# Gate and up GEMMs of the four FFNs by Strassen's seven products instead of eight, one NeuronCore of a Trainium2

## The reference

```python
def swiglu(x, w_gate, w_up, w_down):
    return (jax.nn.silu(x @ w_gate) * (x @ w_up)) @ w_down

x = x + 0.5 * rmsnorm(swiglu(rmsnorm(x, gains[0]), w_gate, w_up, w_down), gains[1])
```

## Time and profile before

| | us |
|---|---|
| median of 3 runs | 2648.09 |
| lowest, highest | 2644.64, 2652.86 |
| span of the profiled execution | 2645.6 |
| TensorE busy | 2565.5 (97%) |
| VectorE, ScalarE, GpSimd busy | 1241.8, 873.3, 411.5 |

### The profile page before, as it was taken

The page is one execution under the profiler, slowest core; times in us unless marked ns, Lnnn a source line. Parts: engine busy times, 40 slices in busy tenths (PEclk is TensorE's granted clock), DMA queues, the critical chain, the costliest instruction groups (busy, mean ns, idle before and its releaser), DMA issues.

```text
span 2645.6 us, 51530 instructions
## 1 busy us (share of the span) xinstructions
PE 2565.5 (97%) x20533; PEld 2435.9 (92%) x20533; DVE 1241.8 (47%) x2018; ACT 873.3 (33%) x1542; POOL 411.5 (16%) x602
## 2 busy tenths in 40 slices
PE   8999999998998999999999999999989989999998
PEld 7999999995557999999999999999979969999998
DVE  5444325546664544432444442467546665444423
ACT  4222224114443422222422222344354444222322
POOL 0000003023331200000200000155245532000001
PEclk9999999999999999999999999999999999999999
DMA  4332322348994233233132233223210133322331
GB/s 125 87 89 86 107 82 65 81 130 287 299 307 152 64 88 88 87 103 88 56 88 87 87 106 90 65 65 87 67 35 1 33 105 96 88 87 87 101 88 45
DMA packets 397765, 263.17 MB, mean 99 GB/s; under 512 B 10984, under 2 KB 370613, under 8 KB 397608
## 3 DMA queue, kind: packets, MB, share of 16 engines
q1 hardware_dynamic: 386096, 223.03, 29.0%
q0 software_dynamic: 11536, 38.28, 4.4%
HBM read 251.71 MB, written 9.56 MB: 99 GB/s over the span
## 4 chain that ended last, share of the span: by engine, by line
PE 90%; DVE 3%; issue 2%; ACT 2%; POOL 2%; DMA 1%; POOLq 0%; SPq 0%; ACTq 0%; DVEq 0%
PE ps L495 70%; PE ps L481 5%; PE ps L1445 2%; PE ps L2391 2%; PE ps L2407 1%; PE ps L1502 1%; PE ps L1457 1%; POOL xT L1026 1%; PE ps L509 1%; PE ps L538 1%; PE ps L2415 1%; PE ps L1468 1%; DVE w_lo L473 0%; DVE rstd_rows L1051 0%; PE ps L2375 0%
## 5 line engine op out<-in xcount | busy, mean ns | idle before, releaser
L473 DVE TENSOR_TENSOR w_lo<-w_raw,w_hi 128x1024 fp32r<-128x1024 f32 (+1 forms) x314 | 423.4, 1348 | 971.3 <-ACT w_hi L466 969.5
L495 PE MATMUL ps<-hd_hi,w_hi 128*128 128x272 f32 x3712 | 772.0, 289 | 4.4 <-DVE w_lo L473 4.3
L495 PE MATMUL ps<-hd_lo,w_hi 128*128 128x272 f32 x3712 | 768.3, 288 | 0.0
L495 PE MATMUL ps<-hd_hi,w_lo 128*128 128x272 f32 x3712 | 762.7, 287 | 0.0
L466 ACT CAST w_hi<-w_raw 128x1024 fp32r<-128x1024 f32 (+1 forms) x314 | 351.4, 1119 | 1124.8 <-PE ps L495 1069.3
L495 PEld LDWEIGHTS ps<-hd_hi,w_hi 128*128 128x128 f32 x3712 | 580.8, 189 | 7.8 <-issue 7.6
L495 PEld LDWEIGHTS ps<-hd_lo,w_hi 128*128 128x128 f32 x3712 | 585.0, 189 | 0.0
L495 PEld LDWEIGHTS ps<-hd_hi,w_lo 128*128 128x128 f32 x3712 | 582.8, 188 | 0.0
L1026 POOL TENSOR_TENSOR xT<-xT,rstd_rows 128x272 f32<-128x272 f32 x96 | 84.5, 910 | 1708.3 <-DVE rstd_rows L1051 1708.2
L495 PE MATMUL ps<-h_hi,w_hi 128*128 128x272 f32 x1232 | 255.4, 289 | 0.0
L495 PE MATMUL ps<-h_lo,w_hi 128*128 128x272 f32 x1232 | 254.9, 288 | 0.0
(11 more groups left out here) (529 smaller groups left out, 2973.7 us busy)
## 6 DMA issues: line engine op xcount, KB each, us to landing
w_raw<-in_ffn_w_gate_dram SPq DMA_DIRECT2D x88, 512.0 KB, 3.7
w_raw<-in_ffn_w_up_dram SPq DMA_DIRECT2D x88, 512.0 KB, 3.8
w_raw<-in_ffn_w_down_dram SPq DMA_DIRECT2D x64, 704.0 KB, 4.6
v_pages<-in_cache_a_v_dram POOLq DMA_DIRECT2D x128, 256.0 KB, 4.5
w_raw<-in_c_w_in_dram SPq DMA_DIRECT2D x33, 512.0 KB, 4.0
k_pages<-in_cache_a_k_dram SPq DMA_DIRECT2D x64, 256.0 KB, 4.2
k_pages_raw<-in_cache_a_k_dram SPq DMA_DIRECT2D x64, 256.0 KB, 4.4
w_raw<-in_ab_w_in_dram SPq DMA_DIRECT2D x25, 512.0 KB, 3.9
```

Source lines behind the costliest of these rows:

```text
L473: e.tensor_tensor(w_lo[:, n % 2, 0:nk * P], raw[:, n % RAW, 0:nk * P], w_hi[:, n % 2, 0:nk * P].bitcast(F32), ALU.subtract).then_inc(sem(" ...
L495: mm = e.matmul(ps[:, bank + h, 0:TH], w, x[:, k0 + k, half(h)], start=first and k == 0 and w is wh and x is x_hi, stop=last and k == nk - ...
```

## The change

The first gate tile and the first up tile of each FFN (four units, 192 matmuls) stay as they were. The other 20 tiles of gate and of up are taken as 10 pairs each. One *pass* p (p = 0 to 19, even: gate pair, odd: up pair) multiplies a 2 x 2 block matrix of weights (two halves of K = 4 k tiles, two output tiles) with a 2 x 2 block matrix of rows (two halves of K, two halves of T) by Winograd's form of Strassen's scheme: seven products instead of eight, each 4 k tiles x 3 passes = 12 matmuls into one bank.

- **Rows.** Strassen adds up results of both halves of the rows, so they must have their 1/rms first. DVE computes 16 tiles `xn` = xT * gain * rb (128 x 272) into `x_sums`, GpSimd four sums of 128 x 1088 (`x_sum` 0 to 3), ACT and DVE split seven operands of 128 x 1088 (`x_part` 0 to 6). All this once for each FFN.
- **Weights.** Two DMAs of 512 KB bring the 128 x 8 x 256 block of a pass to `w_pair` (two buffers). GpSimd makes four sums of 128 x 512 (`w_sum`). ACT and DVE split the seven weight operands (`part`, 128 x 512) into a ring of five slots: part q+5 is made when product q is done.
- **Results.** Seven additions each pass: ACT copies product 0 out of PSUM (`p1`), DVE does `u_sum`, `w_sum`, `quarter` (128 x 272 each) and `sums` (128 x 544), two additions happen in PSUM (products 4 and 6 accumulate onto a bank that holds an earlier result, 5 too), ACT handles `corner`. After each odd pass a silu of 128 x 816 (`gates`) and a product of 128 x 1088 (`gated`) on DVE, for pairs 1 to 4 the split of 128 x 1088 (`pair_high` on ACT, `pair_low` on DVE); the last 12 tiles of the hidden rows are kept whole and split at the end of the stage (`late`), since the row operands occupy their place.
- The loop is written out; one semaphore for each engine counts all its steps of an FFN in a fixed order.

```diff
+PRODUCTS = (("a11", 0), ("s2", 1), ("s1", 3), ("s3", 2), ("a12", 0), ("s4", 3), ("a22", 2))
+        def pool_gate_up(e, g):
+            for n, (to, a, b, op) in enumerate(((2, 3, 6, ALU.add), (1, 2, 0, ALU.subtract), (3, 0, 3, ALU.subtract),
+                                                (5, 4, 1, ALU.subtract))):
+                wait_step(e, "vector", f, "xn", (7, 11, 11, 15)[n])
+                if n:
+                    wait_step(e, "gpsimd", f, "x_sum", n - 1)
+                e.tensor_tensor(x_sums[:, to, :, :], x_sums[:, a, :, :], x_sums[:, b, :, :],
+                                op).then_inc(sem("ffn_gpsimd"), did("gpsimd", "x_sum", n))
+            for p in range(WP):
...
+                pair_landed(e, f, p)
+                b11, b12, b21, b22 = (w_pair[x][:, k:k + KH, m:m + P] for k in (0, KH) for m in (0, P))
+                t3, t2 = (part_rows(w_sums[x][:, y, :]) for y in range(2))
+                e.tensor_tensor(t3, b22, b12, ALU.subtract).then_inc(sem("ffn_gpsimd"), did("gpsimd", "w_sum", 4 * p))
+                wait_step(e, "gpsimd", f, "w_sum", 4 * p)
+                e.tensor_tensor(t2, t3, b11, ALU.add).then_inc(sem("ffn_gpsimd"), did("gpsimd", "w_sum", 4 * p + 1))
+                e.tensor_tensor(b12, b12, b11, ALU.subtract).then_inc(sem("ffn_gpsimd"), did("gpsimd", "w_sum", 4 * p + 2))
...
+                wait_step(e, "vector", f, "part", PROD * p + 1)
+                e.tensor_tensor(t2, b21, t2, ALU.subtract).then_inc(sem("ffn_gpsimd"), did("gpsimd", "w_sum", 4 * p + 3))
+        def pe_product(e, g, q):
...
+            if name == "s4":
+                wait_step(e, "vector", f, "w_sum", p)
+            if name == "a22":
+                wait_step(e, "vector", f, "quarter", p)
+            wait_step(e, "vector", f, "part", q)
+            for k in range(KH):
+                for w, x in ((wh, xp_hi[idx]), (wh, xp_lo[idx]), (wl, xp_hi[idx])):
+                    mm = e.matmul(ps[:, bank, 0:TH], w[:, k * P:(k + 1) * P], x[:, k, :],
...
+        def dve_gate_up(e, g, s):
...
+            dve_rstd_x(e, s, first + 2)
+            dve_split(e, first + 3, 0, KD)
+            gate(0)
+            for h, parts in ((1, (3, 6)), (0, (0, 4))):
+                for k in range(KD):
+                    e.scalar_tensor_tensor(x_sums[:, parts[k // KH], k % KH, :], xT[:, k, half(h)], gain(l, n_pre, k),
+                                           rb[:, half(h)], ALU.mult, ALU.mult
+                                           ).then_inc(sem("ffn_vector"), did("vector", "xn", (1 - h) * KD + k))
+            up(0)
+            hidden(0)
+            low(0)
+            for n in range(3):
+                dve_x_part(e, g, n)
+            gate(1)
+            for q in range(3):
+                dve_part(e, g, q)
+            for n in (3, 4):
+                dve_x_part(e, g, n)
+                dve_part(e, g, n)
+            for q in range(PROD * WP):
+                p, idx = q // PROD, q % PROD
+                pairs = p // 2
+                product_done(e, f, q)
+                dve_sums(e, f, p, idx)
+                if idx == 0 and p % 2 == 0 and p:
+                    dve_gated(e, f, pairs)
+                if idx == 2 and p % 2 == 0 and 0 < pairs < LATE // 2:
...
+                if q + RING < PROD * WP:
+                    dve_part(e, g, q + RING)
+                if q < 2:
+                    dve_x_part(e, g, 5 + q)
+                if q == 0:
+                    up(1)
+                if q == 2:
+                    hidden(1)
+                if q == 4:
+                    low(1)
...
+            dve_gated(e, f, HP)
```

More of the change, by code:

```diff
@@ L568, in quads, with vector_steps @@
                 body(g["quads"] - 1, True)
-        def gate_up_count(g):
-            return KF * ffns.index((int(g["name"][-2]), int(g["name"][-1])))
+        def vector_steps():
+            steps = [("gate", 0), *(("xn", x) for x in range(2 * KD)), ("up", 0), ("hidden", 0), ("low", 0)]
+            steps += [*(("x_part", n) for n in range(3)), ("gate", 1), *(("part", q) for q in range(3))]
+            steps += [("x_part", 3), ("part", 3), ("x_part", 4), ("part", 4)]
+            for q in range(PROD * WP):
+                p, idx = q // PROD, q % PROD
+                steps += [(x, p) for x in {1: ("u_sum",), 2: ("w_sum",), 3: ("quarter",), 6: ("sums",)}.get(idx, ())]
+                steps += [("gated", p // 2)] * (idx == 0 and p % 2 == 0 and p > 0)
+                steps += [("pair_low", p // 2)] * (idx == 2 and p % 2 == 0 and 0 < p // 2 < LATE // 2)
+                steps += [("part", q + RING)] * (q + RING < PROD * WP)
+                steps += [("x_part", 5 + q)] * (q < 2) + [("up", 1)] * (q == 0) + [("hidden", 1)] * (q == 2) + [("low", 1)] * (q == 4)
+                steps += [("late", x) for x in late_at(q) if q < PROD * WP - 1]
+            return steps + [("gated", HP)] + [("late", x) for x in range(7, KF - LATE)]
@@ L603, in act_gate_up, with dve_late @@
+        def dve_late(e, f, x):
+            wait_step(e, "scalar", f, "late", x)
+            e.tensor_tensor(h_hi[:, LATE + x, :], h_raw[:, LATE + x, :], h_lo[:, LATE + x, :].bitcast(F32),
+                            ALU.subtract).then_inc(sem("ffn_vector"), did("vector", "late", x))
         def act_gate_up(e, g, s):
-            m0 = gate_up_count(g)
+            f, first = ffn_of(g), g["first"]
             if s == 0:
                 e.preload_act_table(ACT.Silu)
[L608 to L621, removed]
@@ new lines, in act_gate_up, with dve_gated @@
+            act_split(e, first + 5, 0, KU)
+            for x in range(9, KF - LATE):
+                act_late(e, f, x)
+        def dve_gated(e, f, i):
+            p = 2 * (i - 1)
+            wait_step(e, "vector", f, "sums", p + 1)
+            wait_step(e, "scalar", f, "gates", i)
+            wait_step(e, "scalar", f, "corner", p + 1)
+            to = up_buf if i < LATE // 2 else pair_tiles(h_raw, i)
+            e.tensor_tensor(to, gate_buf, up_buf, ALU.mult).then_inc(sem("ffn_vector"), did("vector", "gated", i))
@@ L3229, in _ @@
                 if kind == "ffn":
-                    sp_gemm(e, gemms[f"gate_up{l}{w}"])
-                    sp_gemm(e, gemms[f"down{l}{w}"])
+                    sp_gate_up(e, gemms[f"gate_up{l}{w}"], gemms[f"down{l}{w}"])
+                    sp_gemm(e, gemms[f"down{l}{w}"], after=1)
                 if kind == "ab":
```

350 lines of the change are left out of this document (294 added, 56 removed).

## The result

The changed kernel took 2667.86 us, the median of four runs (2667.11 to 2672.42); the kernel before took 2649.19 us (2644.64 to 2652.86, four runs). The ratio is 1.0072, 95% interval 1.0057 to 1.0087: slower by 0.7%. The forecast was 2642 us and "no change". The profiled span grew by 20.1 us, from 2645.6 to 2665.7 us, where the forecast had -6: the miss to explain is 26 us.

What follows compares the result with a forecast made beforehand. It took the number of TensorE's matmuls as the bound, other engines hidden. Fewer matmuls -120, start +62, first pass +30, even passes +16, clock +6 gave -6 us: 2648.1 to 2642 us, range 2590 to 2700.

Steps and rivals of the forecast that it cites:

- first pass and clock: Pass 0 of each FFN: ends 7.5 us late, 30 us in all, plus 6 us for TensorE's lowered clock after idling.
- rival 1: Gate and up stage: GpSimd's lock on DVE hardly costs; -84, 2564 us; shares 0.40 with less lock and lower terms.
- Start: Before product 0 of each FFN: TensorE idles 15 us, 17 in the first, until U + 27; 62 us over four.
- Even passes: Passes 2, 4, 6, 8: `quarter` some 1.0 us late, `w_sum` in time; 16 us over four FFNs.
- estimate of 2663 us: Start and passes: whole GpSimd instruction taken as the lock on DVE, +21 us, 2663 us.
- What costs nothing: End of the stage and waits: DVE and ACT free after product 134, down's first splits covered, satisfied waits free; 0 us.
- so I keep 125 ns: Products in all passes: matmuls keep the earlier trace's 125 ns, 1.5 us a product, 10.5 us a pass.
- up to 3 us each FFN: Start of down: the cost if its first unit's 8.3 us no longer covered DVE's work of about 5 us.
- Rival 2: All passes: DVE becomes the bound throughout; +116, 2758 us in full, about 2675 in part; shares 0.38 for slower.
- Rival 3: Start of each FFN: row sums of 2.7 us and a longer low clock; +31, 2673 us; shares 0.38 for slower.
- Rival 4: Products: matmuls fall out of time, for instance from fetching written-out code; 2% slower pace, +19 us; shares 0.38.
- terms that come out higher: Whole sum: the forecast's own terms larger than priced; shares the 0.38 for slower with rivals 2 to 4.

Runs made afterwards that it cites:

- Experiment six: The kernel with all sums small, with every product computed twice over, 24 matmuls instead of 12: a pass takes 21.19 us, a product 3.027 us.
- all sums small: The changed kernel with each of GpSimd's row and weight sums made on one column only, output not the network's: span 2588.9 us.
- the fastest kernel: Changed kernel with two direct column pairs, all sums on DVE in spread order, even passes reordered, old first pass: 2592.23 us, 0.9774 of the kernel before.

## Why the prediction was wrong

The terms of the forecast against the trace of the changed kernel, sums over four FFNs in us:

| term | forecast | measured |
|---|---|---|
| 960 matmuls fewer | -120 | -120 |
| idle before product 0 | 62 | 62.8 (17.3, three of 15.2, without the last matmul's own time) |
| first pass and clock | 36 | 36.3 |
| passes 2, 4, 6, 8 | 16 | 14.9 |
| matmul pace in the other 19 passes | 0 | 7.1 (19 x 0.093 x 4) |
| end of the stage | 0 | 7.5 (0.7, 1.9, 1.9, 2.9) |
| down | 0 | 2.9 |
| other passes late (pass 1, even passes from 10 on) | 0 | 5.0 |
| everything else | 0 | 3.6 |
| sum | -6 | +20.1 |

**What was right.** The mechanism, and the sum of each term that was worked out. The exclusion between the engines was priced at 2642 - 2564 = 78 us by the forecast and its rival 1; taking it away gave 76.8 us. Inside the terms several steps were off and cancelled, and that is luck:

- *Start.* I had GpSimd's first sum push in between the `xn`, and it was the other way round. A row sum also held DVE for 2.3 us (3.56 - 1.28), not for 1.8: it takes 2.5 us rather than my 2.0, as the least disturbed ones show (2.51 us, in the kernel with two direct pairs and GpSimd's sums). In return one weight sum and a part of the second, instead of three, came ahead of product 0. So the start still fell on U + 27.0.
- *First pass and clock.* 36 was 30 of waits and 6 of clock. By the starts of the matmuls in pass 0 it was some 22 us of waits and 13 us lost by matmuls at the lower clock: the first product's 12 starts spread over 2.63 us instead of 1.39, and after the waits of 2.4 and 2.5 us ahead of products 4 and 5 the clock was low once more (0.66 from 1365 to 1370 us).
- *Even passes.* `quarter` was late, but by 0.5 to 0.75 us instead of 1.0; `w_sum`, which I had in time, was late too, by 0.1 to 0.6 us in 12 of the 16.

The prediction's estimate of 2663 us, with a weight sum's lock of 1.27 instead of 1.15 us, lies near the measured time for another reason: alternating with sums a low part takes 1.78 instead of 0.68 us, so the lock is 1.1 us, and the 26 us lie elsewhere.

**The step that failed** is "What costs nothing", with "so I keep 125 ns". All of the 26 us lies in terms put at zero, or left out of the sum:

- *The end.* "parts stop at product 134, so DVE and ACT are free": they are, but down's first split writes into buffers that the last products read. In the third FFN ACT can start it only when the last product but one is done, and ACT's half and DVE's half take 1.37 and 1.63 us in a row, 3 us with 1.5 us of matmuls left. In the fourth FFN the load of down's first unit has to wait for the last part too:

```profile
2508.84 1.37 ACT L499 CAST w_hi<-w_raw 128x1408 fp32r<-128x1408 f32 x1 [2.11 <-DMA w_raw<-in_ffn_w_down_dram]
2510.31 1.62 DVE L506 TENSOR_TENSOR w_lo<-w_raw,w_hi 128x1408 fp32r<-128x1408 f32 x1 [3.33 <-ACT w_hi L499]
```

  My "up to 3 us each FFN" was about another wait, the splits that come while down reads its first unit; that the gaps, 0.7 to 2.9 us, lie within it is chance. Gaps of 0.7 to 4.5 us stand there in the kernels without GpSimd's sums too, so they are no part of the exclusion. Experiment six tests the cause without having been made for it: with the last product 1.51 us longer, the gaps of 0.7, 1.9, 1.9 and 2.7 us that it had with products of 12 matmuls become 0, 0.4, 0.4 and 0. In the second and third FFN that is just the 1.51 us by which the two splits are covered longer.
- *The pace.* 7.1 us, from the earlier trace rows taken over to another form of matmul sequence. That it is a price per matmul is shown; why is open.
- *Late passes.* From pass 10 on 12 of the 20 even passes take 10.83 to 11.05 us. `quarter` is in time there, as I had it; what is late is `w_sum`, ahead of product 5, by 0.15 to 0.36 us. With sums of one column no pass is late, so this belongs to the exclusion.
- *Down.* It is 0.34 us longer three times and 1.86 us once, in the fourth FFN, behind the gap of 2.9 us. There the granted clock fell (column 7), while behind the 1.9 us of the third FFN it stayed at 1.00:

```profile
2512.00:2516.00 4.00, 3.92 (x20) 3.95 (x21) 3.96 (x6) 2.92 (x5) 0.00 (x0) 0.62 1.20 290
```

```profile
1583.00:1587.00 4.00, 4.00 (x33) 4.00 (x34) 3.97 (x6) 3.01 (x5) 0.00 (x0) 1.00 1.00 262
```

  20 matmuls in 4 us instead of 33 are the 1.5 us: a short stall had cost half of its length again. The length of the stall does not decide it alone: with all sums small, gaps of 1.9 us in the second and third FFN were followed by a clock of 0.57 over 4 us, and down took 136.3 instead of 134.8 us. The 0.34 us and the 3.6 us elsewhere in the program are not explained.

**The rivals.** Rival 1 is false: the exclusion costs all that the rows said, and even without it the kernel takes 2590.7 us, not 2564. Of the 27 us between the two, 20 are again the terms costed at nothing (pace 7.1, end 7.3, down 5.7), 3 are pass 0 (13.84 us instead of 13.0) and 2 the gaps (28.1 instead of 26). Rival 2 did not come: the odd passes are on time at 10.59 to 10.84 us. Rival 3: the start is as forecast, though its longer row sums were half true; the granted clock of pass 0, 0.81, is inside the first pass's 36 us. Rival 4 has the effect, at 0.9% instead of 2%, but not the reason: written-out direct units keep their 125.0 ns. The chance of 0.38 for "slower" named mechanisms 2 to 4; what came is covered only by its "terms that come out higher", a sum of small ones. A sum of four large terms that nearly cancel has to be as good as its smallest ones; "nothing" five times over was the weakest part of it.

## What to carry to other kernels

Work moved to GpSimd is not free for DVE: a sum of 512 columns that DVE does itself in 0.60 us costs it about 1.1 us when GpSimd does it beside DVE instructions with two SBUF inputs, so here DVE was better off doing the very work that had been taken from it. When TensorE waits at the start of a stage for preparations, a few units of direct matmuls put ahead are cheap cover: 3 us of matmuls more in each FFN took the gap from 15.3 to 1.5 us and the whole span from 2665.7 to 2642.3 us, though part of the gap moved into the first pass. And when a forecast is a difference of large terms, list every place where buffers change owner (the end of a stage above all) and price each; a "free" engine is not yet a free buffer.

## What the runs showed of the hardware

- DVE's run of 16 instructions back to back (6.69 us) was not slowed by a GpSimd instruction that was ready from 1335.32 us on and waited. Once in turns, a 128x544 instruction took 2.23 instead of 0.73 us and three 128x1088 ones 9.31 instead of 3.69 us. GpSimd needs no pause of DVE to get in: here the low part follows `gated` without one and takes 1.78 instead of 0.68 us. ACT's half of that part was done at 1387.93, ahead of its start.

```profile
1387.15 1.28 DVE L906 TENSOR_TENSOR scratch<-scratch 128x1088 f32<-128x1088 f32 x1
1388.35 1.78 DVE L795 TENSOR_TENSOR part_lo<-w_pair,part_hi 128x512 fp32r<-128x512 f32 x1
1387.29 2.30 POOL L720 TENSOR_TENSOR w_sums<-w_pair 128x512 f32<-128x512 f32 x1 [1.84 <-DMA w_pair<-in_ffn_w_up_dram]
```

  The 16 `xn` wait for nothing between them, while the low part has a wait for ACT, already met. Whether this is what lets GpSimd in was not tested.
- The costs of the exclusion add up within 1 us: row sums 29.4, weight sums 48.4, both 76.8 us, one run each.
- Matmuls of the same shape ran at 125.0 ns each in one sequence (direct units) and at 126.1 ns in another (products), steadily, at a granted clock of 1.00 in both.
- In the third FFN, with a gap from 1340.3 to 1355.5, the granted clock was 0.50 (the lower of the two levels, 1.2 GHz) at 1350 to 1355 us, 0.57 at 1355 to 1360, 1.00 at 1360 to 1365 and 0.66 at 1365 to 1370, where TensorE waited again. In the fastest kernel, with a gap of 0.8 us there and one of 4.4 in pass 0, that pass has 0.90. A gap of 2.9 us at the end of the stage brought 0.62 for 4 us, one of 1.9 us in the same kernel brought nothing, and one of 1.9 us in the kernel with all sums small brought 0.57 for 4 us.
